# Compressed projections with both precision parts in one stationary operand, and their two halves moved among the gate groups

## The chip, the cores and the metric

The kernel runs on one core of a Trainium2 chip. The metric is the device time of one execution in microseconds; the time given is the median of three runs. TensorE multiplies, VectorE and GpSimd do elementwise work, ScalarE does activations and copies, and SyncE issues the loads of the weights.

## The reference, cut to what matters

The reference is one decoder block of two layers with 512 tokens and a model width of 1024. The change touches one piece of its sparse attention, the compressed keys and values:

```python
def compress_blocks(x, pos, w1, w2):
    ...
    blocks = jnp.concatenate([xs[:, i:i + nc] for i in range(r)], axis=2)
    blocks = blocks + pos[:, None, :]
    flat = jnp.moveaxis(blocks, 3, 2).reshape(B, nc, G, CMP_LEN * d)
    return jax.nn.gelu(flat @ w1) @ w2
```

It is called once for keys and once for values. There are 31 blocks of 32 tokens in each of 2 groups of heads with 64 channels, so `flat` has 62 rows (64 with padding) of 2048 numbers, and `w1` is 2048 x 256. What follows it on the same inputs is attention over the compressed blocks, over selected blocks and over a window, then `g_a * (ya @ w_a2d) + g_b * (yb @ w_b2d)`, whose gates `g_a` and `g_b` are sigmoids of further projections.

## The kernel before

**Precision.** A product of float32 matrices is computed in three matmuls. Every operand is split into a high part, rounded to the matmul's format, and a low part, the rest. The sum of high times high, high times low and low times high is accumulated in one bank of PSUM.

**The stream of weights.** All weight matrices lie in one stream of 128 x 128 tiles, cut into slabs of 8 tiles, in the order in which TensorE uses them (`dense_layers`, from L53). SyncE loads slab s into one of 4 raw slots (L635) as soon as slab s - 4 has been split. ScalarE rounds the slab to `w_hi` (`feed_to`, L1408 to L1416), into one of 5 slots, as soon as TensorE has used slab s - 5. Then GpSimd subtracts and gets `w_lo` (L676). From the third slab of the compressed projection on, four slabs (`DVE_SLABS`, every second one) have their `w_lo` made by VectorE instead (L2328). TensorE waits for `w_lo` at the first tile of a slab (`weight`). ScalarE's rounding is not a queue of its own: calls of `feed(name)` in ScalarE's program round all slabs up to three behind the last slab of `name`, and `after_group(name)` does that and then waits for the group's last matmul. Whatever ScalarE waits for in between holds back the slabs behind it.

**Order on TensorE around the change.** It is written out by hand (L1343 to L1347): `dense_tokens("nv", 2)`, then `compress_keys()`, `compressed(1)`, and `nsa()`.
- `compressed(b)` (L1061 to L1077) is the product `flat @ w1`, for keys (b = 0) and values (b = 1). The activations are the stationary operand: for each of 16 pairs of tiles 128 x 64 of `zc_hi` or `zc_lo`, while 256 columns of the weights move past. The output is 64 partitions x 256 columns. There are 48 matmuls for each b, 32 with `zc_hi` and 16 with `zc_lo`, over four slabs.
- `fill(p)` is a piece of work put between others: p = 0 and 1 are the halves of the gate group `gate_a0`, 2 and 3 of `gate_a1`, 4 and 5 are the groups `a2d0` and `a2d1`. Each has 12 matmuls of 512 columns. All these groups write PSUM bank 7, one after the other, and each waits until its predecessor was read: `gate_a` by a Tanh of ScalarE (`nsa_gate`, L1756), `a2d` by VectorE's `mix_down` (L2402).
- `hidden(b)` transposes the result of the Gelu, `hid_copy` moves it to SBUF, and 8 small matmuls multiply with `w2`.
- `scores`, `turn` and `values` are the steps of attention. `scores(s + 2)` waits for VectorE's `biased(s)` (`m_done`), `turn(s)` for VectorE's scaled probabilities (`p_done`).

The order is: compressed keys, fill 0, `hidden(0)`, fill 1, keys' small products, compressed values, `scores(0)`, `scores(1)`, `hidden(1)`, fill 2, values' small products, fill 3, `scores(2)`, `scores(3)`, fill 4, `turn(0)`, fill 5, and so on.

**Order on ScalarE** (L1705 to L1783): round slabs up to 30, copy the four `nv` results, `hid_gelu(0)` (which first rounds slabs 31 to 33, L1709 to L1712), round on for `gate_a0`, `hid_copy(0)`, Tanh of `gate_a0`, copy of the compressed keys, `hid_gelu(1)` with rounding before it, a one-column Exp that loads the table, `hid_copy(1)`, the exponentials of steps 0 and 1, copy of the compressed values, Tanh of `gate_a1`.

**Order on VectorE** (L2320 to L2420): `zc_lo` twice, `ya_lo` four times, the four slabs of `DVE_SLABS`, then `biased(0)` (for step 0 this is `cmp_front`: two additions from PSUM, a maximum, and the subtraction at L2345), `biased(1)`, `cmp_back(0)`, and for every step s `inverted`, `biased(s + 2)`, `scaled`, `mix_down`.

Of the kernel before, what the change touches and what calls it, by code (L numbers as in the profile page):

```python
# [19 lines left out]
ALU = mybir.AluOpType  # L20
# [33 lines left out]
def dense_layers():  # L54
# [4 lines left out]
         ("cmpk", 1, 16, 2), ("gate_a0", 1, 8, 0), ("cmpv", 1, 16, 2), ("gate_a1", 1, 8, 0)]  # L59
# [74 lines left out]
def build(nc, t):  # L134

    ctx = ExitStack()
    with ctx:
# [86 lines left out]
        zc = arena("zc", 40, [2, 16, NG, 32])  # L224
        zc_hi = arena("zc_hi", 32, [2, 16, NG, 32], F32R)
        zc_lo = arena("zc_lo", 40, [2, 16, NG, 32], F32R)
# [166 lines left out]
        hid_act = sem("hid_act")  # L393
        hid_tr = sem("hid_tr")
# [96 lines left out]
        frees("cmpk", hid_act, [1])  # L491
        frees("cmpv", hid_act, [2])
# [60 lines left out]
        first = START["cmpk"][0] // SLAB  # L553
        DVE_SLABS = range(first + 2, last_slab[START["cmpv"][1]] + 1, 2)
# [22 lines left out]
        bank_of[START["cmpk"][1]], bank_of[START["cmpv"][1]] = 3, 6  # L577
# [104 lines left out]
        def _(pe):  # L682
# [364 lines left out]
            def fill(p):  # L1047
                if p < 3 * DC:
                    m, r = p // 6 * 2, p % 6
                    if r < 4:  # L1050
                        for i in range(4 * (r % 2), 4 * (r % 2) + 4):
                            dense_part(f"gate_a{m + r // 2}", 0, i, u_hi, u_lo)
                    else:
                        for i in range(4):
                            dense_part(f"a2d{m + r - 4}", 0, i, ya_hi, ya_lo, 4)
# [5 lines left out]
            def compressed(b):  # L1061

                tile, g = START[("cmpk", "cmpv")[b]]
                pe.wait_ge(zc_ready, b + 1)
                wait_bank(g)
                out = psum[bank_of[g]][0:64, 0:256]
                for i in range(16):
                    hi, lo = weight(tile, 2)
                    zh = zc_hi[:, b, i, :, :].rearrange("p a b -> p (a b)")
                    zl = zc_lo[:, b, i, :, :].rearrange("p a b -> p (a b)")  # L1070
                    mm(out, zh, hi, start=(i == 0), stop=False)
                    mm(out, zh, lo, start=False, stop=False)
                    last = mm(out, zl, hi, start=False, stop=(i == 15))
                    tile += 2
                    if i < 15:
# [10 lines left out]
            def compress_keys():  # L1086

                compressed(0)
                fill(0)
                pe.wait_ge(nv_done, NT)  # L1090
                hidden(0)
                fill(1)
# [5 lines left out]
                last.then_inc(hid_tr, 1)  # L1098

            def compress_values():  # L1100

                hidden(1)
                fill(2)
# [6 lines left out]
                fill(3)  # L1110

            def nsa():
# [56 lines left out]
                pe.wait_ge(nv_done, 4)  # L1169
                scores(0)  # L1170
# [174 lines left out]
            compressed(1)  # L1345
            pe.wait_ge(ya_ready, 4)
# [57 lines left out]
        def _(act):  # L1404
# [294 lines left out]
            for b in range(2):  # L1699
                act.wait_ge(zc_sum, 2 * b + 2)  # L1700
                f(zc_hi[:, b, :, :, :], zc[:, b, :, :, :], ACT.Copy).then_inc(zc_part, 1)
# [80 lines left out]
            nsa_gate(3)  # L1782
# [244 lines left out]
        def _(dve):  # L2027
# [292 lines left out]
            for b in range(2):  # L2320
                dve.wait_ge(zc_part, b + 1)
                TT(zc_lo[:, b, :, :, :], zc[:, b, :, :, :], zc_hi[:, b, :, :, :].bitcast(F32), ALU.subtract)\
# [532 lines left out]
```

## Time and profile before

| | us |
|---|---|
| median of three runs | 2185.66 (2185.46 to 2186.32) |
| the profiled execution, its own time | 2185.49 |
| its span (first to last instruction) | 2183.7 |
| TensorE busy | 2145.4 |
| VectorE, ScalarE, GpSimd busy | 883.9, 878.9, 902.1 |

The profile is of one execution. All times in it are from the start of its span. A matmul's row gives its own duration, from entering to leaving the array; in a row of matmuls the distance from start to start is what one costs. An instruction's idle time stands in brackets behind it, with what ended it. The granted clock of TensorE is at its upper level (0.998 of full speed) in the mean over the whole span.

### The profile page before, as it was taken

The numbers are of one execution on the slowest core, as the hardware profiler recorded it, in microseconds if no ns is written. First come the engines' busy times: TensorE is split into PE (matmuls) and PEld (weight loads), VectorE is DVE, ScalarE is ACT, GpSimd is POOL, SyncE is SP. The second block draws the span as 40 slices with busy tenths as digits, with TensorE's granted clock in tenths as the row PEclk, the third lists the DMA queues.
The fourth block names the chain that finished last, engine by engine and source line by source line (L and its number), as shares of the span: only waits on it lengthen the run. The fifth ranks groups of instructions, "written<-read, shape, count | busy, mean of one in ns | idle before, by whom it ended". The sixth has DMA issues, their size and how long they took to land.

```text
span 2183.7 us, 27219 instructions
## 1 busy us (share of the span) xinstructions
PE 2145.4 (98%) x10960; PEld 1757.7 (80%) x10960; DVE 883.9 (40%) x1588; ACT 878.9 (40%) x1471; POOL 902.1 (41%) x385
## 2 busy tenths in 40 slices
PE   7999999999999999999999999999999999999998
PEld 6788877787788888788888888778788888888886
DVE  5494645346655500463332114653644132333211
ACT  5544655544444422452222232662346233222321
POOL 3332322245544443654444444043524444444432
PEclk9999999999999999999999999999999999999999
DMA  5222321142333333223333323023322333333321
GB/s 167 85 68 88 120 67 50 59 135 78 97 97 97 103 102 103 87 77 97 97 97 97 106 87 110 22 80 104 108 81 68 99 96 93 97 97 97 106 96 48
DMA packets 56141, 200.03 MB, mean 92 GB/s; under 512 B 6480, under 2 KB 7376, under 8 KB 55632
## 3 DMA queue, kind: packets, MB, share of 16 engines
q1 hardware_dynamic: 52416, 188.77, 28.3%
q10 hardware_dynamic: 3600, 9.53, 1.3%
q8 instruction: 87, 1.43, 0.3%
q14 instruction: 38, 0.31, 0.0%
HBM read 194.07 MB, written 2.10 MB: 90 GB/s over the span
## 4 chain that ended last, share of the span: by engine, by line
PE 92%; DVE 4%; ACT 2%; POOL 1%; issue 1%; DMA 0%; ACTq 0%; DVEq 0%
PE dense L769 16%; PE dense L771 16%; PE dense L770 16%; PE misc L769 5%; PE misc L770 5%; PE misc L771 5%; PE misc L713 3%; PE misc L715 2%; PE misc L714 2%; PE dense L749 2%; PE dense L752 2%; PE dense L753 2%; PE dense L713 1%; PE dense L715 1%; PE dense L714 1%; PE dense L1128 1%
## 5 line engine op out<-in xcount | busy, mean ns | idle before, releaser
L676 POOL TENSOR_TENSOR w_lo<-raw,w_hi 128x1024 fp32r<-128x1024 f32 x348 | 852.5, 2463 | 1161.3 <-ACT w_hi L1415 1138.2
L1415 ACT ACTIVATE w_hi<-raw 128x1024 fp32r<-128x1024 f32 x352 | 362.2, 1051 | 149.4 <-PE dense L771 87.3
L769 PE MATMUL dense<-u_hi,w_hi 128*128 128x512 f32 x848 | 333.1, 393 | 2.7 <-POOL w_lo L676 1.6
L771 PE MATMUL dense<-u_hi,w_lo 128*128 128x512 f32 x848 | 330.0, 389 | 0.0
L770 PE MATMUL dense<-u_lo,w_hi 128*128 128x512 f32 x824 | 320.7, 389 | 0.0
L769 PE MATMUL dense<-a_hi,w_hi 128*128 128x512 f32 x528 | 206.2, 391 | 0.0
L771 PE MATMUL dense<-a_hi,w_lo 128*128 128x512 f32 x528 | 205.4, 389 | 0.0
L770 PE MATMUL dense<-a_lo,w_hi 128*128 128x512 f32 x528 | 205.4, 389 | 0.0
L769 PEld LDWEIGHTS dense<-u_hi,w_hi 128*128 128x128 f32 x848 | 159.2, 188 | 38.0 <-issue 3.7
L771 PEld LDWEIGHTS dense<-u_hi,w_lo 128*128 128x128 f32 x848 | 159.2, 188 | 33.1
L770 PEld LDWEIGHTS dense<-u_lo,w_hi 128*128 128x128 f32 x824 | 154.7, 188 | 33.3 <-issue 1.4
L769 PE MATMUL misc<-u_hi,w_hi 128*128 128x512 f32 x424 | 166.0, 391 | 0.0
L771 PE MATMUL misc<-u_hi,w_lo 128*128 128x512 f32 x424 | 165.0, 389 | 0.0
L770 PE MATMUL misc<-u_lo,w_hi 128*128 128x512 f32 x416 | 161.9, 389 | 0.0
L769 PEld LDWEIGHTS dense<-a_hi,w_hi 128*128 128x128 f32 x528 | 99.1, 188 | 21.0 <-issue 0.5
L770 PEld LDWEIGHTS dense<-a_lo,w_hi 128*128 128x128 f32 x528 | 99.1, 188 | 21.0 <-issue 0.5
L771 PEld LDWEIGHTS dense<-a_hi,w_lo 128*128 128x128 f32 x528 | 99.1, 188 | 20.6
L2114 DVE SCALAR_TENSOR_TENSOR h<-dense,h 128x512 f32<-128x512 f32 x24 | 16.6, 692 | 223.7 <-PE dense L771 223.7
L2068 DVE TENSOR_TENSOR slot<-slot,slot 128x512 f32<-128x512 f32 x58 | 48.5, 837 | 135.0 <-ACT slot L1504 133.5
L1523 ACT ACTIVATE slot<-dense 128x512 f32<-128x512 f32 x30 | 17.9, 598 | 205.4 <-DVE dense L2097 205.4
L769 PEld LDWEIGHTS misc<-u_hi,w_hi 128*128 128x128 f32 x424 | 79.6, 188 | 17.1 <-issue 0.5
L771 PEld LDWEIGHTS misc<-u_hi,w_lo 128*128 128x128 f32 x424 | 79.6, 188 | 16.6
(472 smaller groups left out, 3819.3 us busy)
## 6 DMA issues: line engine op xcount, KB each, us to landing
raw<-in_weights SPq DMA_DIRECT2D x352, 512.0 KB, 3.6
h<-in_x SPq DMA_DIRECT2D x4, 512.0 KB, 5.7
alibi<-in_alibi ACTq DMA_DIRECT2D x1, 2048.0 KB, 8.6
h<-in_x ACTq DMA_DIRECT2D x2, 1024.0 KB, 6.8
out<-result SPq DMA_DIRECT2D x8, 256.0 KB, 2.2
hn<-mqk ACTq DMA_DIRECT2D x4, 256.0 KB, 4.0
mqk<-mqk ACTq DMA_DIRECT2D x4, 256.0 KB, 3.5
masks_in<-in_masks ACTq DMA_DIRECT2D x1, 512.0 KB, 4.1
```

The source lines that it names most:

```text
L676: nc.gpsimd.tensor_tensor(w_lo[:, s % SPLITS, :, :], raw[:, s % RAWS, :, :], w_hi[:, s % SPLITS, :, :].bitcast(F32), ALU.subtract).then_in ...
L713: mm(out, hi, src_hi[:, i, :], start=(i == 0), stop=False)
L714: mm(out, hi, src_lo[:, i, :], start=False, stop=False)
L715: last = mm(out, lo, src_hi[:, i, :], start=False, stop=(i == k - 1))
L749: first = mm(out, hi, src_lo[:, i, :], start=(i == 0), stop=False)
L752: mm(out, hi, src_hi[:, i, :], start=False, stop=False)
L753: last = mm(out, lo, src_hi[:, i, :], start=False, stop=(i == k - 1))
L769: mm(out, hi, src_hi[:, i, :], start=(i == 0), stop=False)
L770: mm(out, hi, src_lo[:, i, :], start=False, stop=False)
L771: last = mm(out, lo, src_hi[:, i, :], start=False, stop=(i == k - 1))
L1415: f(w_hi[:, s % SPLITS, :, :], raw[:, s % RAWS, :, :], ACT.Copy).then_inc(w_part, 1)
L2068: TT(slot[2][:, :], (slot[2] if c > 1 else sq[0])[:, :], sq[c % 3][:, :], ALU.add).then_inc(ms_acc, 1)
```

## The change

The low and high parts of the activations are put side by side: `zc_both` holds for each tile pair 64 columns of the high and 64 of the low part, and is one stationary operand of 128 x 128. Each compressed projection then has 32 matmuls, 16 with `w_hi` and 16 with `w_lo`, and its output has 128 partitions: the high part's product in partitions 0 to 63, the low part's in 64 to 127. (The product of low and low parts, left out before, is now in the sum.) ScalarE copies the lower half to `hid_low`, VectorE adds it to the upper half in PSUM, and then Gelu reads it.

The stream has each projection cut in two, `cmpk0`, `cmpk1`, `cmpv0`, `cmpv1`, two slabs each, with the gate groups between: `cmpk0`, `gate_a0`, `cmpk1`, `cmpv0`, `gate_a1`, `cmpv1`. TensorE's order follows: half keys, fill 0, fill 1, half keys, half values, `hidden(0)`, fill 2, keys' small products, fill 3, half values, `scores(0)`, `scores(1)`, two of the four tiles of fill 4, `hidden(1)`, `scores(2)`, `scores(3)`, values' small products, the other two tiles of fill 4, `turn(0)`, fill 5 and so on. ScalarE's and VectorE's orders change as shown.

```diff
-         ("cmpk", 1, 16, 2), ("gate_a0", 1, 8, 0), ("cmpv", 1, 16, 2), ("gate_a1", 1, 8, 0)]
+         ("cmpk0", 1, 8, 2), ("gate_a0", 1, 8, 0), ("cmpk1", 1, 8, 2), ("cmpv0", 1, 8, 2), ("gate_a1", 1, 8, 0),
+          ("cmpv1", 1, 8, 2)]
...
-        zc = arena("zc", 40, [2, 16, NG, 32])
-        zc_hi = arena("zc_hi", 32, [2, 16, NG, 32], F32R)
-        zc_lo = arena("zc_lo", 40, [2, 16, NG, 32], F32R)
+        zc = arena("zc", 16, [2, 16, NG, 32])
+        zc_both = arena("zc_both", 32, [2, 16, 2, NG, 32], F32R)
+        hid_low = arena("hid_low", 64, [2, 256])
...
-        first = START["cmpk"][0] // SLAB
-        DVE_SLABS = range(first + 2, last_slab[START["cmpv"][1]] + 1, 2)
+        first = START["cmpk0"][0] // SLAB
+        DVE_SLABS = range(first + 2, last_slab[START["cmpv1"][1]] + 1, 2)
...
-            def fill(p):
+            def fill(p, tiles=range(4)):
...
-                        for i in range(4):
+                        for i in tiles:
                             dense_part(f"a2d{m + r - 4}", 0, i, ya_hi, ya_lo, 4)
...
-            def compressed(b):
-
-                tile, g = START[("cmpk", "cmpv")[b]]
-                pe.wait_ge(zc_ready, b + 1)
-                wait_bank(g)
-                out = psum[bank_of[g]][0:64, 0:256]
-                for i in range(16):
+            def compressed(b, half):
+
+                tile, g = START[("cmpk", "cmpv")[b] + str(half)]
+                if half == 0:
+                    pe.wait_ge(zc_ready, b + 1)
+                    wait_bank(g)
+                out = psum[bank_of[g]][:, 0:256]
+                for i in range(8 * half, 8 * half + 8):
                     hi, lo = weight(tile, 2)
-                    zh = zc_hi[:, b, i, :, :].rearrange("p a b -> p (a b)")
-                    zl = zc_lo[:, b, i, :, :].rearrange("p a b -> p (a b)")
-                    mm(out, zh, hi, start=(i == 0), stop=False)
-                    mm(out, zh, lo, start=False, stop=False)
-                    last = mm(out, zl, hi, start=False, stop=(i == 15))
+                    z = zc_both[:, b, i, :, :, :].rearrange("p a b c -> p (a b c)")
+                    mm(out, z, hi, start=(i == 0), stop=False)
+                    last = mm(out, z, lo, start=False, stop=(i == 15))
...
-                compressed(0)
+                compressed(0, 0)
                 fill(0)
+                fill(1)
+                compressed(0, 1)
+                compressed(1, 0)
                 pe.wait_ge(nv_done, NT)
                 hidden(0)
-                fill(1)
+                fill(2)
                 pe.wait_ge(hid_done, 1)
...
                 last.then_inc(hid_tr, 1)
+                fill(3)
+                compressed(1, 1)

             def compress_values():

-                hidden(1)
-                fill(2)
                 pe.wait_ge(hid_done, 2)
...
-                fill(3)
...
                 scores(0)
                 scores(1)
-                compress_values()
-                pe.wait_ge(kvc_copied, 2)
+                fill(4, range(2))
+                hidden(1)
                 for first in range(0, SLOTS, 2):
                     if first + 2 < SLOTS:
                         scores(first + 2)
                         scores(first + 3)
                     alone = first % 9 == 0
+                    if first == 0:
+                        compress_values()
                     for s in (first, first + 1):
                         if s < SLOTS - 1:
-                            fill(pieces_of(s)[0])
+                            fill(pieces_of(s)[0], range(2, 4) if s == 0 else range(4))
+                        if s == 0:
+                            pe.wait_ge(kvc_copied, 2)
                         turn(s)
...
             def hid_gelu(b):
-                name = ("cmpk", "cmpv")[b]
+                name = ("cmpk1", "cmpv1")[b]
                 after_group(name)
+                f(hid_low[0:64, b, :], out_bank(name)[64:128, 0:256], ACT.Copy).then_inc(hid_moved, 1)
+                act.wait_ge(hid_sum, b + 1)
                 f(hid_t[0:64, b, :], out_bank(name)[0:64, 0:256], ACT.Gelu_apprx_tanh).then_inc(hid_act, 1)
...
+            feed("gate_a0")
+            nsa_gate(1)
+            f(spare_col, one_col, ACT.Gelu_apprx_tanh)
             hid_gelu(0)
-            feed("gate_a0")
+            feed("cmpv0")
             hid_copy(0)
-            nsa_gate(1)
             act.wait_ge(hid_tr, 2)
             f(kc[:, :], misc[0][:, 0:32], ACT.Copy).then_inc(kvc_copied, 1)
+            nsa_gate(3)
             hid_gelu(1)
...
-            nsa_gate(3)
             nsa_feed(1)
...
+            def hid_add(b):
+
+                dve.wait_ge(hid_moved, b + 1)
+                out = out_bank(("cmpk1", "cmpv1")[b])[0:64, 0:256]
+                TT(out, out, hid_low[0:64, b, :], ALU.add).then_inc(hid_sum, 1)
+
             for s in DVE_SLABS:
+                if s > last_slab[START["cmpv0"][1]] and s - 2 <= last_slab[START["cmpv0"][1]]:
+                    hid_add(0)
                 dve.wait_ge(w_part, s + 1)
...
+            hid_add(1)
             dve.wait_ge(c_loaded, 80)
             biased(0)
```

## Rows read from the trace of the kernel before

**Rows 1.** The page, busy time of each engine, and the chain that ended last:

```profile
PE 2145.4 (98%) x10960; PEld 1757.7 (80%) x10960; DVE 883.9 (40%) x1588; ACT 878.9 (40%) x1471; POOL 902.1 (41%) x385
...
PE 92%; DVE 4%; ACT 2%; POOL 1%; issue 1%; DMA 0%; ACTq 0%; DVEq 0%
```

**Rows 2.** Timeline of TensorE: start and duration in us, instruction, [idle before <- releaser]:

```profile
223.32 0.28 PE L788 MATMUL misc<-w_hi,u_hi 128*128 128x256 f32 x1
...
234.83 0.28 PE L1071 MATMUL dense<-w_hi,zc_hi 128*64 128x256 f32 x1
...
238.84 0.33 PE L1071 MATMUL dense<-w_hi,zc_hi 128*64 128x256 f32 x1 [1.12 <-DVE w_lo L2328]
...
242.27 0.47 PE L713 MATMUL misc<-u_hi,w_hi 128*128 128x512 f32 x1 [0.47 <-DVE w_lo L2328]
...
248.94 0.33 PE L1071 MATMUL misc<-w_hi,zc_hi 128*64 128x256 f32 x1
...
254.53 1.08 PE L1122 MATMUL dense<-kc,nq 64*128 64x31 f32 x16
...
255.75 0.28 PE L1083 MATMUL misc<-ident,hid_t 64*128 64x64 f32 x2
...
258.92 0.63 PE L1107 MATMUL misc<-w,hid 128*32 128x64 f32 x8
...
263.18 0.50 PE L713 MATMUL misc<-ya_hi,w_hi 128*128 128x512 f32 x1
...
266.03 1.03 PE L1141 MATMUL misc<-ident,c_s 128*31 128x128 f32 x8
266.97 0.50 PE L713 MATMUL misc<-ya_hi,w_hi 128*128 128x512 f32 x1
```

**Rows 3.** Timeline of ScalarE, same columns, from slab 33 to slabs 35 to 38:

```profile
242.48 1.06 ACT L1415 ACTIVATE w_hi<-raw 128x1024 fp32r<-128x1024 f32 x1 [4.55 <-DMA raw<-in_weights]
243.56 1.28 ACT L1712 ACT_TABLE_LOAD   x1
244.85 0.38 ACT L1712 ACTIVATE hid_t<-dense 64x256 f32<-64x256 f32 x1
...
248.69 0.60 ACT L1756 ACTIVATE gate_t<-misc 128x512 f32<-128x512 f32 x1 [2.35 <-PE misc L715]
...
249.26 4.07 ACT L1415 ACTIVATE w_hi<-raw 128x1024 fp32r<-128x1024 f32 x4
```

**Rows 4.** Timeline of VectorE, same columns, first steps of attention:

```profile
255.73 0.48 DVE L2340 TENSOR_TENSOR c_s<-dense,c_bias 128x124 f32<-128x124 f32 x2 [4.16 <-PE dense L1122]
...
256.69 2.10 DVE L2345 TENSOR_TENSOR c_s<-c_s,st 128x248 f32<-128x248 f32 x1
...
259.27 0.41 DVE L2352 TENSOR_REDUCE st<-c_s 128x8 f32<-128x248 f32 x1
...
260.94 0.16 DVE L2381 RECIPROCAL st<-st 128x2 f32<-128x2 f32 x1
262.96 0.29 DVE L2371 CUSTOM_DVE_ANT_0 n_s<-dense,alibi 128x128 f32<-128x128 f32 x1 [1.86 <-PE dense L1128]
...
263.39 0.60 DVE L2392 TENSOR_SCALAR n_s<-n_s,st,small 128x128 f32<-128x128 f32 x2
266.23 0.69 DVE L2402 SCALAR_TENSOR_TENSOR mix_t<-gate_t,misc 128x512 f32<-128x512 f32 x1 [2.24 <-PE misc L715]
```

**Rows 5.** Two lines of VectorE: durations in ns (least, median, most), first and last start:

```profile
L2328 DVE TENSOR_TENSOR w_lo<-raw,w_hi x4: 1224/2318/3439, 235.4 to 250.3; 128x1024 fp32r<-128x1024 f32 x4
...
L2345 DVE TENSOR_TENSOR c_s<-c_s,st x4: 417/1094/2102, 256.7 to 374.9; 128x248 f32<-128x248 f32 x4
```

**Rows 6.** Timeline of GpSimd, slab 34:

```profile
246.26 2.40 POOL L676 TENSOR_TENSOR w_lo<-raw,w_hi 128x1024 fp32r<-128x1024 f32 x1 [5.21 <-ACT w_hi L1415]
```

**Rows 7.** Timelines of GpSimd and VectorE, from 523 to 538 us:

```profile
527.59 10.37 POOL L676 TENSOR_TENSOR w_lo<-raw,w_hi 128x1024 fp32r<-128x1024 f32 x4 [4.42 <-ACT w_hi L1415]
...
523.64 9.71 DVE L2068 TENSOR_TENSOR slot<-slot,slot 128x512 f32<-128x512 f32 x7
```

More of the change, by code:

```diff
@@ L393, in build @@
         hid_act = sem("hid_act")
+        hid_moved = sem("hid_moved")
+        hid_sum = sem("hid_sum")
         hid_tr = sem("hid_tr")
@@ L490, in build @@
         frees("nv", nv_done, [1, 2, 3, 4])
-        frees("cmpk", hid_act, [1])
-        frees("cmpv", hid_act, [2])
+        for b in range(2):
+            frees(f"cmpk{b}", hid_act, [1])
+            frees(f"cmpv{b}", hid_act, [2])
         for m in range(DC):
@@ L576, in build @@
             bank_of[START["nv"][1] + c] = 4 + c
-        bank_of[START["cmpk"][1]], bank_of[START["cmpv"][1]] = 3, 6
+        for b in range(2):
+            bank_of[START[f"cmpk{b}"][1]], bank_of[START[f"cmpv{b}"][1]] = 3, 6
         for name in ("up", "up1", "up2"):
@@ L1059, in fill @@
                         dense_part(f"gate_b{m}", 0, i, u_hi, u_lo)
-            def compressed(b):
-                tile, g = START[("cmpk", "cmpv")[b]]
-                pe.wait_ge(zc_ready, b + 1)
-                wait_bank(g)
-                out = psum[bank_of[g]][0:64, 0:256]
-                for i in range(16):
-                    hi, lo = weight(tile, 2)
-                    zh = zc_hi[:, b, i, :, :].rearrange("p a b -> p (a b)")
-                    zl = zc_lo[:, b, i, :, :].rearrange("p a b -> p (a b)")
-                    mm(out, zh, hi, start=(i == 0), stop=False)
-                    mm(out, zh, lo, start=False, stop=False)
-                    last = mm(out, zl, hi, start=False, stop=(i == 15))
+            def compressed(b, half):
[5 more added lines that the diff above has]
+                for i in range(8 * half, 8 * half + 8):
+                    hi, lo = weight(tile, 2)
+                    z = zc_both[:, b, i, :, :, :].rearrange("p a b c -> p (a b c)")
+                    mm(out, z, hi, start=(i == 0), stop=False)
+                    last = mm(out, z, lo, start=False, stop=(i == 15))
                     tile += 2
-                    if i < 15:
+                    if i % 8 < 7:
                         used(last, tile - 1)
@@ L1169, in nsa @@
                 pe.wait_ge(nv_done, 4)
+                pe.wait_ge(ya_ready, 4)
                 scores(0)
                 scores(1)
-                compress_values()
-                pe.wait_ge(kvc_copied, 2)
+                fill(4, range(2))
+                hidden(1)
                 for first in range(0, SLOTS, 2):
@@ L1344, in _ @@
             compress_keys()
-            compressed(1)
-            pe.wait_ge(ya_ready, 4)
             nsa()
@@ L1700, in _ @@
                 act.wait_ge(zc_sum, 2 * b + 2)
-                f(zc_hi[:, b, :, :, :], zc[:, b, :, :, :], ACT.Copy).then_inc(zc_part, 1)
+                f(zc_both[:, b, :, 0, :, :], zc[:, b, :, :, :], ACT.Copy).then_inc(zc_part, 1)
             for hd in range(GH):
@@ L2321, in _ @@
                 dve.wait_ge(zc_part, b + 1)
-                TT(zc_lo[:, b, :, :, :], zc[:, b, :, :, :], zc_hi[:, b, :, :, :].bitcast(F32), ALU.subtract)\
+                TT(zc_both[:, b, :, 1, :, :], zc[:, b, :, :, :], zc_both[:, b, :, 0, :, :].bitcast(F32), ALU.subtract)\
                     .then_inc(zc_ready, 1)
@@ L2739, in layout @@
         "ncmp": np.concatenate([kcm, vcm], 1),
-        "nv": np.concatenate([vsl, vwi], 1), "cmpk": one("cmp_w1_k"), "cmpv": one("cmp_w1_v"),
+        "nv": np.concatenate([vsl, vwi], 1),
+        "cmpk0": one("cmp_w1_k")[:D], "cmpk1": one("cmp_w1_k")[D:],
+        "cmpv0": one("cmp_w1_v")[:D], "cmpv1": one("cmp_w1_v")[D:],
         "w_o": one("w_o"), "up": pairs(up[:, :FF], up[:, FF:]), "down": one("w_down"),
```

## The prediction

> **What bounds the kernel now.** I read the page first. TensorE is busy 98% of the span and 92% of the chain that ended last is its own work [rows 1]. So a microsecond off TensorE's own stream counts in full, but so does every new wait in that stream. The sum is made on the profiled execution: span 2183.7 us, time 2185.49 us, which is 0.17 us under the median of 2185.66 us. An effect in that one stretch is carried to the median unchanged. 0.2% of it is 4.4 us, about what a measurement of this kernel can tell from no change.
>
> Then the stretch that the edit touches, from the first compressed matmul at 234.83 us to the point where the second `a2d` group starts, 266.97 us: 32.14 us [rows 2]. Behind that point the order of the work is the old one. TensorE's timeline shows what a matmul costs there: with 128 stationary columns 96 matmuls of 256 moving columns take from 223.32 to 234.83 us, 0.120 us each; with 64 stationary columns 48 of them take from 248.94 to 254.53 us, 0.116 us each with the gap behind, 0.114 us from start to start. It idles 1.12 us at 238.84 and 0.47 us at 242.27 us, both for a `w_lo` slab that VectorE makes [rows 2]. Everything else in the stretch is back to back.
>
> Last the engines that feed it, because the change moves their work too. ScalarE rounds a slab in 1.06 us, or four in 4.07, and loads a table for Gelu in 1.28 us, between slab 33 at 242.48 and the Gelu at 244.85 us [rows 3]. GpSimd makes a `w_lo` slab in 2.4 us [rows 6], VectorE one in 1.22 us at best and in 3.4 us at worst, beside GpSimd [rows 5]. In the old numbering slabs 27 to 30 are `cmpk`, 31 `gate_a0`, 32 to 35 `cmpv`, 36 `gate_a1`, 37 the first two `a2d`. In the new one 27 and 28 are `cmpk0`, 29 `gate_a0`, 30 and 31 `cmpk1`, 32 and 33 `cmpv0`, 34 `gate_a1`, 35 and 36 `cmpv1`, 37 as before. VectorE's slabs stay 29, 31, 33 and 35.
>
> **What goes.** 96 matmuls at 0.114 us become 64 at 0.120 us: 10.94 less 7.68, a saving of 3.3 us. That a full-width stationary costs double is excluded by the 0.120 us [rows 2]. With it the wait of 0.47 us goes, as slab 31 is now needed after a whole gate group.
>
> **What comes, as a clock.** Up to 242 us nothing ahead of ScalarE, VectorE and GpSimd has changed, so old times hold for slabs 29 to 32.
> - 234.83: `cmpk0`, 16 matmuls, to 236.75. Slab 29 is ready at 238.79, as now; TensorE waits 2.1 us, 0.8 more than now (counted from start to start). `gate_a0`, 24 matmuls of 512 columns with 0.23 us each ([rows 2]: 12 take 2.85 us from 263.18 to 266.03), to 244.4; its result is whole at 244.65.
> - `cmpk1` and slab 32 of `cmpv0`, 24 matmuls, to 247.3.
> - ScalarE now issues `feed("gate_a0")`, which ends with slab 32, and then stands in the wait of `nsa_gate(1)` until 244.65. Slab 33, rounded at 242.48 now [rows 3], is queued behind it. Tanh 0.6, to 245.3; table load for the spare Gelu 1.28, to 246.6; slab 33 from 246.7 to 247.75; slab 34 to 248.7. Only an extra load for Tanh stands ahead of its wait, in idle time. VectorE makes slab 33 by 249.0. TensorE waits **1.7 us**, then does its 8 matmuls to 250.0.
> - The halves: ScalarE's copy of 64x256, 0.39 (the Gelu of the same shape, [rows 3]), VectorE's addition some 0.35 (between 0.24, half of the `c_s<-dense` pair of 124 columns, and 0.69, `mix_t` with 512 columns, both with a PSUM operand, [rows 4]), Gelu 0.39: done about 249.8, covered by `cmpv0`. Without that cover it would cost 1.1 us.
> - Slab 34 (`gate_a1`) is GpSimd's: from 248.75 to 251.15. TensorE is through the two transposes at 250.3 and waits **0.9 us**. Two fills and the 8 small products of the keys take it to 257.25; `gate_a1` is whole at 257.4. `cmpv1` to 259.2, its slabs being ready. `scores(0)` and `(1)`, 1.22 us (254.53 to 255.75, [rows 2]), to 260.4.
> - ScalarE waits in `nsa_gate(3)` until 257.4; Tanh to 258.0; then slabs 37, 38 and 39 to 260.95, before it copies the lower half of `cmpv1`. GpSimd makes slab 37 from 259.1 to 261.5: TensorE waits **1.1 us** for it. Half of `a2d0` and the two transposes, to 263.3.
> - VectorE adds the halves at 261.65 and only then starts `biased(0)`, which now runs at 255.73 [rows 4]: 0.96 us to the subtraction `c_s<-c_s,st`. This reads SBUF twice; at 256.69 it took 2.10 us beside GpSimd [rows 4], against 0.42 us at best [rows 5]. Here it waits for slab 38, until 263.9, and ends at 264.2. `scores(2)` needs it: TensorE waits **0.9 us**. `scores(2)` and `(3)`, the values' products (0.63), the other half of `a2d0`: to 267.15.
> - `biased(1)` 0.5, to 264.75; `cmp_back(0)` takes 1.67 us (259.27 to 260.94, [rows 4]) and is held once more by slab 39, until 266.6: done 267.65. `turn(0)` waits **0.5 us** for it.
> - `inverted(1)`, `biased(2)`, `scaled(1)` 1.2 us (0.16, and 262.96 to 263.99, [rows 4]), then `mix_t` of `a2d0` 0.69: 269.45. The second `a2d` group needs that bank: TensorE, through `turn(0)` at 268.6, waits **0.8 us**.
>
> So the second `a2d` group starts at 269.45, not 266.97: **2.5 us later**. As a check: 3.3 and 0.5 saved; 0.8, 1.7, 0.9, 1.1, 0.9, 0.5 and 0.8 added, 6.7 in all, less 3.8, is 2.9. I take the clock. Buffers: the two raw and split rings have the same slots, and by the clock no load is late, since slab 33's has landed by 242.48 and the others start when the slab four before is split.
>
> ScalarE's load takes 1.28 us and its next instruction follows at once: load at 243.56, Gelu at 244.85 [rows 3]. The Trainium skill (ScalarE: Activation LUTs, "What ACT_TABLE_LOAD costs") adds a drain of 1.38 us to each switch, 2.66 us in all; by it slab 33 would come 1.4 us later and the kernel be at 2189.5. The trace does not agree, and the sum keeps 1.28.
>
> **The rivals.**
> - *The saving arrives.* If ScalarE's slabs 33, 34 and 37 are not needed as early as I have them, only slab 29's wait stays: 3.3 and 0.5 less 0.8, 3.0 us faster, 2182.7. For it: the new order is easier on the feed per matmul, and GpSimd has idle time, 5.21 us before slab 34 [rows 6]. Against: ScalarE's instruction order is fixed, and slab 33 stands behind Tanh in it.
> - *No table load between Tanh and slab 33*, since now Tanh runs at 248.69 in Gelu's table without a load [rows 3]. The set that serves Tanh first may be that one. Then everything from slab 33 on is 1.4 us earlier: +1.1, 2186.8.
> - *Slower.* VectorE's subtraction at 262.6 meets GpSimd with slab 39 queued right behind slab 38. If GpSimd keeps the access, VectorE starts at 266.3, 2.4 us later, and so do `turn(0)` and all behind it: +4.9, 2190.6. It decides once ScalarE rounds slab 39 before 263.9; by the clock it does. Against: around 530 us VectorE's `slot<-slot,slot` got in between two of GpSimd's four queued slabs, which then took 10.37 us in place of four times 2.4 [rows 7]. By the Trainium skill (SBUF — State Buffer, "Who interferes with whom") whoever issues first holds the shared port for the whole instruction; the trace agrees, with 2.10 us for the subtraction of 0.42.
>
> **How the numbers follow.** Forecast 0.60, saving arrives 0.12, no load 0.13, slower 0.15. The likeliest gives 2185.66 + 2.5 = 2188.2 us. The terms that no row gives exactly (addition 0.24 to 0.69, load 0 or 1.28, one hand-over of 2.4) span -1.4 to +2.4 about it, 2186.8 to 2190.6. I put the range at 2184.6 to 2190.9: it leaves out the first rival and what lies beyond the last. Faster by over 0.2% would need more than the whole saving: 0.02. Slower by over 0.2% is the last rival: 0.15. The rest, 0.83, is within 0.2%.
>
> **What would show it.** After: 32 matmuls of each compressed projection, 0.120 us apart; TensorE idle some 2 us before `gate_a0`, 1.7 us inside `cmpv0` for VectorE's slab, 0.9 us before `gate_a1` and 1.1 us before `a2d0`, both for GpSimd's; ScalarE's slab 33 starting near 246.7, behind Tanh and a table load; `biased(0)` not before 261 us. The forecast is wrong if slab 33 is rounded before Tanh, if TensorE does not wait in `cmpv0`, or if the second `a2d` group starts before 266.5 us.

## The result, and the profile after

The changed kernel takes 2196.64 us (median of 5 runs, 2195.32 to 2197.04) against 2185.58 us (5 runs, 2184.99 to 2186.32): 11.06 us more, a ratio of 1.0048 [1.0037, 1.0059]. Forecast was 2188.2 us, between 2184.6 and 2190.9. The profiled execution took 2197.04 us with a span of 2195.2 us, the one before 2183.7 us.

The page after, the same two lines as [rows 1]:

```profile
PE 2148.4 (98%) x10928; PEld 1759.4 (80%) x10928; DVE 883.9 (40%) x1590; ACT 881.1 (40%) x1475; POOL 902.7 (41%) x385
...
PE 92%; DVE 4%; ACT 2%; POOL 1%; issue 1%; DMA 0%; ACTq 0%; DVEq 0%
```

There are 32 matmuls fewer, as the change says, and yet TensorE is busy 3.0 us longer. The other 8.5 of the 11.5 us by which the span is longer are idle time. Shares of the span can't tell where; three views do. The first is a yardstick that both kernels have: the moments at which ScalarE rounds each of the 352 slabs. The kernel after lags the one before by 0.75 us at slab 28 (ahead of any changed instruction), 4.43 at slab 40, then by the same until slab 112, 9.48 at slab 118, 11.27 at slab 200, 12.23 at slab 230, 11.56 at slab 300 and to the end. So the changed stretch cost 3.7 us, and 7.1 us were lost in steps of 5.1, 1.8, 1.0 and -0.7 in places that the diff doesn't touch. The second view names them: what TensorE waited for from 700 to 1900 us, before,

```profile
engine line waited for: us in total, times, longest us
PE misc L1210 <- ACT w_pt L1878: 1.3, 2, 0.8
PE dense L788 <- ACT r_raw L1934: 1.0, 1, 1.0
```

and after, in the same stretch:

```profile
engine line waited for: us in total, times, longest us
PE dense L774 <- DVE slot L2479: 3.2, 1, 3.2
PE dense L774 <- DVE slot L2114: 1.5, 1, 1.5
PE misc L1221 <- ACT w_pt L1891: 1.3, 2, 0.8
...
PE dense L741 <- issue: 0.8, 1, 0.8
```

The line for `w_pt` has its twin before. The other three, for L774 twice and for L741, have none: they are new. TensorE's timeline after, start and duration in us, with the idle time ahead in brackets:

```profile
239.66 0.47 PE L718 MATMUL misc<-u_hi,w_hi 128*128 128x512 f32 x1 [1.99 <-DVE w_lo L2349]
...
251.40 0.39 PE L1076 MATMUL misc<-w_hi,zc_both 128*128 128x256 f32 x1 [1.54 <-DVE w_lo L2349]
...
253.73 0.47 PE L718 MATMUL misc<-u_hi,w_hi 128*128 128x512 f32 x1 [0.84 <-POOL w_lo L681]
...
264.18 0.47 PE L718 MATMUL misc<-ya_hi,w_hi 128*128 128x512 f32 x1 [0.93 <-POOL w_lo L681]
...
271.45 0.50 PE L718 MATMUL misc<-ya_hi,w_hi 128*128 128x512 f32 x1 [0.29 <-DVE mix_t L2423]
...
756.23 0.39 PE L776 MATMUL dense<-u_hi,w_lo 128*128 128x512 f32 x1
...
759.79 0.79 PE L774 MATMUL dense<-a_hi,w_hi 128*128 128x512 f32 x1 [3.17 <-DVE slot L2479]
...
1191.02 0.50 PE L774 MATMUL dense<-a_hi,w_hi 128*128 128x512 f32 x1 [1.51 <-DVE slot L2114]
1311.83 0.47 PE L741 MATMUL dense<-u_hi,w_hi 128*128 128x512 f32 x1 [0.83 <-issue]
```

The first five are the waits of the changed stretch, and they answer to the forecast's clock. (The row at 756.23 us has no wait; it is the last matmul of `up`.) The last three are not in it at all: the first matmuls of `down`, of `down1` and of the `wq` part. Ahead of `down` the kernel before went straight on:

```profile
751.81 0.39 PE L771 MATMUL dense<-u_hi,w_lo 128*128 128x512 f32 x1
752.03 0.39 PE L769 MATMUL dense<-a_hi,w_hi 128*128 128x512 f32 x1
```

The reason is one line of the code that the diff does not touch, `bank_of = [g % 4 for g in range(GROUPS)]`: a group's PSUM bank comes from its number. The change cuts `cmpk` and `cmpv` into two groups each, so every group behind them has a number that is two higher and, where the code gives it no bank by hand, sits two banks away from its old one. The up projection in front of `down` doesn't move: its 44 groups count their own six banks (`c % 6`). Before, `down`'s first group took over bank 3, last used by group 39 of `up`; now it takes bank 1, that of group 43, the last one, and so waits for VectorE's last step of the convolution (L2479). Before, the four groups of `up` that came behind group 39 covered that step. `down1` meets the same behind `up1`. The first group of `wq` has bank 0 by hand; before, it took that bank over from the third last group of `down1`, now from the last one. The row of its wait names no releaser, but the wait comes and goes with the banks in the first two experiments.

The third view, windows at four moments (us, then busy time and count of instructions of PE, PEld, DVE, ACT and POOL, then PEclk, DMA share, GB/s):

```profile
189.78:193.20 3.42, 3.42 (x18) 3.42 (x18) 0.23 (x1) 2.33 (x4) 3.42 (x2) 0.50 0.58 150
240.98:244.40 3.42, 3.42 (x10) 2.65 (x9) 1.85 (x1) 0.00 (x0) 0.76 (x1) 0.50 0.93 304
264.88:268.29 3.41, 3.41 (x18) 2.33 (x18) 2.86 (x9) 2.73 (x8) 3.41 (x2) 0.50 0.72 189
759.81:763.22 3.41, 3.41 (x8) 2.73 (x9) 1.82 (x3) 0.78 (x2) 0.00 (x0) 0.50 0.00 0
```

The granted clock is 0.50 in each: TensorE runs at 1.2 instead of 2.4 GHz. Three of the four falls begin within 1.4 us behind a wait of the timeline above (1.99, 0.93 and 3.17 us). The first stands in unchanged code, and TensorE waited at most 0.23 us at a time in the 5 us ahead of it. Eight matmuls fill 3.41 us from 759.81 us, 0.43 us each. In the kernel before, at full clock, 63 of them fill 14 us there, 0.22 us each:

```profile
752.00:766.00 14.00, 14.00 (x63) 11.59 (x62) 8.21 (x8) 7.73 (x10) 6.49 (x3) 1.00 0.39 122
```

This fall therefore costs 8 times 0.21, 1.7 us. A fall costs less where it takes the place of a wait. The one at 189.78 us is why the slabs lag by 0.75 us at slab 28 (at slab 27 they do not lag yet): of its 1.3 us of longer matmuls, 0.5 went into a wait that only the kernel before has:

```profile
192.13 0.38 PE L999 MATMUL dense<-u_new,kt_t 128*128 128x128 f32 x1 [0.52 <-ACT u_new L1662]
```

The longer matmuls count as busy time, which is how TensorE can be busy longer with fewer of them. Counted up to the same matmul in both kernels, TensorE was busy 1.2 us longer ahead of the changed stretch, 1.0 behind it, 2.9 behind the fall at 759.81 us and 3.0 at the end. So in the changed stretch its two falls, and what five waits cost beyond their idle time, used up the 3.3 us saved. The profile before shows no fall while TensorE has work.

Two theories stand for the first experiments. By the one, the waits behind the changed stretch come from the banks alone, whatever the order. By the other, the new order itself delays what follows, and the waits near 756 and 1188 us go with it.

### The profile page after: what moved, and what is told of

Read it like the earlier page. It is cut to its first block, busy times and chain, and to the rows that moved or that the text cites. A ratio compares the mean times of both kernels' runs of the same rounds, so it can differ in the third digit from the quotient of the medians.

```text
span 2195.2 us, 27161 instructions
## 1 busy us (share of the span) xinstructions
PE 2148.4 (98%) x10928; PEld 1759.4 (80%) x10928; DVE 883.9 (40%) x1590; ACT 881.1 (40%) x1475; POOL 902.7 (41%) x385
## 4 chain that ended last, share of the span: by engine, by line
PE 92%; DVE 4%; ACT 2%; POOL 1%; issue 1%; DMA 0%; ACTq 0%; DVEq 0%
PE dense L774 16%; PE dense L776 16%; PE dense L775 16%; PE misc L776 5%; PE misc L775 5%; PE misc L774 5%; PE misc L718 3%; PE misc L720 2%; PE misc L719 2%; PE dense L754 2%; PE dense L758 2%; PE dense L757 2%; PE dense L718 1%; PE dense L720 1%; PE dense L719 1%; PE dense L1134 1%
## 5 line engine op out<-in xcount | busy, mean ns | idle before, releaser
L774 PE MATMUL dense<-u_hi,w_hi 128*128 128x512 f32 x848 | 333.2, 393 | 2.7 <-POOL w_lo L681 1.6
L774 PE MATMUL dense<-a_hi,w_hi 128*128 128x512 f32 x528 | 207.2, 392 | 4.7 <-DVE slot L2479 3.2
L774 PEld LDWEIGHTS dense<-u_hi,w_hi 128*128 128x128 f32 x848 | 159.2, 188 | 37.9 <-issue 3.7
L774 PE MATMUL misc<-u_hi,w_hi 128*128 128x512 f32 x424 | 166.0, 391 | 0.0
L774 PEld LDWEIGHTS dense<-a_hi,w_hi 128*128 128x128 f32 x528 | 99.5, 188 | 26.5 <-DVE slot L2479 3.6
L774 PEld LDWEIGHTS misc<-u_hi,w_hi 128*128 128x128 f32 x424 | 79.6, 188 | 17.1 <-issue 0.5
```

The costliest lines, as they stand in the source:

```text
L774: mm(out, hi, src_hi[:, i, :], start=(i == 0), stop=False)
```

## The experiments

The kernel before, run beside them on the same chips, took 2186.00 us (26 runs) with the first four, 2186.07 (31 runs) with the next four, 2186.03 (29 runs) with the last four.

### The old banks, with the whole change

```diff
-        bank_of = [g % 4 for g in range(GROUPS)]
+        bank_of = [(g - 2 * (g > START["cmpv1"][1])) % 4 for g in range(GROUPS)]
```

> The changed kernel, with the PSUM banks of all groups behind the compressed ones numbered as in the kernel before. Bank theory: the 3.2 us wait of TensorE before the first matmul of down at 760 us and the 1.5 us one before down1 at 1191 us come from the group numbers that moved by two, which put these groups into the bank that the last up group still holds. Then both waits go, with the clock drop behind the first, and the time falls by the 7.2 us that the kernel loses after 460 us: 2189.4 us. Rival, chance in the placing of later work (instruction supply, clock): the waits stay, 2196.6 us.

Measured: 2189.74 us (10 runs), 1.0018 [1.0008, 1.0027]. The waits of `down`, `down1` and `wq` are gone, and the lag at the slabs stays at 4.1 us from slab 40 to the end. So of the 11.06 us lost 3.7 are left, and 7.3 came from the banks. The ten runs lie in three groups, 2187.37 and 2187.8, four at 2189.03 to 2189.93, four at 2191.0 to 2191.9, whose means lie 1.9 and 2.0 us apart, near the price of a fall. That reads as runs with none, one and two, but only one of them has a profile: the falls of the others are argued from their times. The profiled execution, 2189.55 us, is of the middle group and has one fall, behind the waits before `gate_a0`, in `cmpv0` and before `gate_a1`:

```profile
252.28:255.69 3.41, 3.41 (x9) 2.65 (x9) 0.44 (x1) 0.14 (x1) 2.61 (x1) 0.50 0.78 259
```

Its timeline of TensorE, from 264 us on, shows what the kernel after hides under its slower clock:

```profile
266.32 0.38 PE L1134 MATMUL dense<-nk,nq 64*128 64x128 f32 x2 [0.63 <-DVE c_s L2366]
...
269.56 0.27 PE L1147 MATMUL misc<-ident,c_s 128*31 128x128 f32 x1 [0.17 <-DVE c_s L2378]
...
271.07 0.50 PE L718 MATMUL misc<-ya_hi,w_hi 128*128 128x512 f32 x1 [0.47 <-DVE mix_t L2423]
```

From the first compressed matmul to the second `a2d` group it takes 35.76 us with this one fall, and the kernel after takes 35.86 us with two: its fall at 264.88 us took the place of the first two of these waits and of part of the third, and cost about 0.1 us. So falls can't simply be counted at 1.7 us each.

### The new banks, with nothing else

```diff
-        bank_of = [g % 4 for g in range(GROUPS)]
+        bank_of = [(g + 2 * (g > START["cmpv"][1])) % 4 for g in range(GROUPS)]
```

This is the kernel before, with each later group in the bank that the change gives it.

> The kernel before, with nothing but the group numbers behind the compressed groups moved by two for the choice of banks. Bank theory: it loses what the changed kernel loses after 460 us, some 7 us, 2192.8 us, with waits of about 3 us before down and 1.5 us before down1. Rival (the waits need the changed stretch): 2185.6 us.

Measured: 2193.4 us (5 runs), 1.0034 [1.0021, 1.0047], 7.4 us more than the kernel before. Without one instruction of the change, both waits are there, at their full length:

```profile
756.10 0.78 PE L769 MATMUL dense<-a_hi,w_hi 128*128 128x512 f32 x1 [3.17 <-DVE slot L2457]
...
1187.37 0.50 PE L769 MATMUL dense<-a_hi,w_hi 128*128 128x512 f32 x1 [1.51 <-DVE slot L2101]
```

The theory of the order falls. Its profile has the fall behind `down`'s wait too. The fastest of the five, 2192.11 us, has a mean granted clock of 0.999 where the others have 0.997; it is 6.1 us above the kernel before, so most of the 7.4 us is waiting and not clock. The 7.4 us here and the 3.7 us of the old banks' run are 11.1, the whole loss of 11.06.

### TensorE kept busy in the wait for slab 29

The old banks, plus 16 matmuls of 256 columns into an unused bank where TensorE waits for slab 29.

```diff
+                for _ in range(16):
+                    mm(bank[1][:, 0:256], zc_both[:, 0, 0, :, :, :].rearrange("p a b c -> p (a b c)"), u_hi[:, 0, 0:256],
+                       start=True, stop=True)
```

> As e1_old_banks, with 16 matmuls of 256 columns into an unused bank in the place where TensorE idles 2 us for slab 29; their result is not used. Clock theory: the granted clock does not fall at 241 us, gate_a0 runs at 0.23 us a matmul throughout, and the time is 1.7 to 1.9 us under e1_old_banks (2187.6 us). Rival, the clock falls for another reason than the idle time, or the fall is covered by the wait for slab 33 behind it: no difference to e1_old_banks, or less than 0.5 us.

Measured: 2189.09 us (10 runs), 0.65 us under the old banks' run and not 1.7: a miss as a median. The group with two falls is gone (none over 2189.58), but only one run, at 2187.56, is in the group with none, and the profiled one has a fall at 251.4 us. Three runs, at 2188.34 to 2188.56, lie between the groups. Keeping this one wait filled removes at most one of the falls.

### VectorE makes slab 29 first

The old banks; VectorE splits slab 29 ahead of the four `ya_lo` steps instead of behind them.

```diff
+            slab_lo(DVE_SLABS[0])
             for hd in range(GH):
                 head_lo(hd)
...
-            for s in DVE_SLABS:
+            for s in DVE_SLABS[1:]:
```

> As e1_old_banks, with VectorE making slab 29 ahead of the four ya_lo subtractions in place of behind them. My clock: slab 29 is ready before TensorE asks, the 2.0 us wait and the 1.8 us of low clock behind it go, and all waits behind move up with it, as their producers hang on gate_a0: 3.8 us under e1_old_banks, 2185.6 us. Rival, the later waits (slab 33 behind Tanh, slab 37, biased) take it back since they hang on loads and GpSimd: 1 us or less.

Measured: 2187.5 us (10 runs), 1.0002 [0.9993, 1.0012]. That is 2.2 us under the old banks' run where 3.8 were expected: a miss as a median. Four runs are at 2184.87 to 2185.32, near the 2185.6 us expected, and six at 2187.32 to 2188.2. The wait before `gate_a0` is gone; those for ScalarE's slabs 33 and 34 (1.54 and 0.85 us) stay, and behind them the profiled run has a fall to 0.50 of 6.83 us, from 248.33 us on, twice as long as the others.

### ScalarE ahead of Tanh

Now the step that the forecast made the main one: slab 33 behind Tanh. On top of the last edit, ScalarE issues the slabs of `cmpk1`'s feed and the spare Gelu before it stands in the wait for `gate_a0`.

```diff
-            feed("gate_a0")
-            nsa_gate(1)
             f(spare_col, one_col, ACT.Gelu_apprx_tanh)
+            feed("cmpk1")
+            nsa_gate(1)
```

> As e4_slab29_first, with ScalarE loading Gelu's table and rounding slabs 33 and 34 ahead of the Tanh of gate_a0 in place of behind it. Queue theory (slab 33 is late because it stands behind the Tanh and a table load in ScalarE's program): the waits of 1.54 us inside cmpv0 and 0.85 us before gate_a1 both go, 2.4 us under the undisturbed runs of e4 (2185.1): 2182.7 us, and the clock has no idle time of over a microsecond to fall on. Rival, slab 33 is late through its load or through VectorE: the 1.54 us stays, 2185 to 2187.5 us.

Measured: 2183.11 us (10 runs), 0.9986 [0.9977, 0.9996]. Both waits are gone, 0.94, 0.65, 0.18 and 0.47 us are left, and the runs lie in one group, 2182.41 to 2184.01 us. (Three of them have a mean granted clock of 0.997 and are no slower than the rest.) Against the lower group of the run before this is 2.1 us less, about the two waits' 2.4; against its median it is 4.4. The difference fits the clock, which does not fall in this profile.

### ScalarE ahead of the second gate too

On top of the last edit, slabs 37 and 38 are rounded ahead of the Tanh of `gate_a1`.

```diff
-                after_group(name)
+                if b == 0:
+                    after_group(name)
+                else:
+                    act.wait_ge(dense_done, group_of(name))
...
+            feed_to(last_slab[START["cmpv1"][1]] + 3)
             nsa_gate(3)
```

> As e5_scalar_ahead, with slabs 37 and 38 rounded ahead of the Tanh of gate_a1, and slab 39 behind the Gelu of the values. Queue theory: the waits of 0.94, 0.65, 0.18 and 0.47 us behind cmpv1 (slab 37, the subtraction of the compressed scores, turn(0), the bank of a2d1) go as well, another 2.2 us: 2180.5 us, 5 us under the kernel before. Rival, the copy, addition and Gelu of two halves are a chain that holds up biased(0) whatever is ahead of it: the waits on VectorE stay, 1 us or less gained over e5.

Measured: 2180.9 us (10 runs), 0.9977 [0.9968, 0.9986]. ScalarE rounds slabs 31 to 34 and only then meets its Tanh:

```profile
236.83 1.28 ACT L1783 ACT_TABLE_LOAD   x1
...
238.24 2.94 ACT L1424 ACTIVATE w_hi<-raw 128x1024 fp32r<-128x1024 f32 x3
243.26 1.06 ACT L1424 ACTIVATE w_hi<-raw 128x1024 fp32r<-128x1024 f32 x1 [2.08 <-PE misc L720]
244.22 0.58 ACT L1770 ACTIVATE gate_t<-misc 128x512 f32<-128x512 f32 x1
```

In the window over these matmuls TensorE's busy time is the window itself, at full clock:

```profile
235.50:262.19 26.69, 26.69 (x183) 22.44 (x181) 14.62 (x30) 17.20 (x35) 14.95 (x6) 1.00 0.65 198
```

From 234 to 280 us one wait is left, the one for `a2d1`'s bank that was expected to go too. In total, times and longest:

```profile
PE misc L718 <- DVE mix_t L2431: 0.5, 1, 0.5
```

### The operand alone

The kernel before with only the shared operand, the copy and the addition of the halves; groups, order and banks as before.

```diff
-                    mm(out, zh, hi, start=(i == 0), stop=False)
-                    mm(out, zh, lo, start=False, stop=False)
-                    last = mm(out, zl, hi, start=False, stop=(i == 15))
+                    mm(out, z, hi, start=(i == 0), stop=False)
+                    last = mm(out, z, lo, start=False, stop=(i == 15))
```

> The kernel before, old order and old groups, with only the operand changed: 32 matmuls with 128 stationary columns for each projection, halves copied and added. My sum: the keys' saving goes into the wait for slabs 29 and 31, which stay ready at 238.8 and 242.1 us, the values keep 1.6 us: 2184.4 us, or about 2186 with a fall of the clock behind the longer wait at 238.8 us. Rival, TensorE saves all of it: 3.3 us, 2182.7 us. Rival, the chain of copy, addition and Gelu is on the path in hidden(1): 2186 to 2187 us without any fall of the clock.

Measured: 2186.0 us (10 runs), 0.9999 [0.9989, 1.0008]. The 3.3 us saved turn into waits:

```profile
239.45 0.39 PE L1072 MATMUL dense<-w_hi,zc_both 128*128 128x256 f32 x1 [1.91 <-DVE w_lo L2338]
...
242.88 0.47 PE L715 MATMUL misc<-u_hi,w_hi 128*128 128x512 f32 x1 [1.25 <-DVE w_lo L2338]
...
246.32 0.24 PE L1083 MATMUL misc<-ident,hid_t 64*128 64x64 f32 x1 [0.44 <-ACT hid_t L1714]
...
255.76 0.27 PE L1083 MATMUL misc<-ident,hid_t 64*128 64x64 f32 x1 [0.48 <-ACT hid_t L1714]
```

The first two grew from 1.12 and 0.47 us [rows 2], 1.6 us more; the other two are the chain of copy, addition and Gelu with nothing over it, 0.9 us. Together 2.5 of the 3.3. In this profile, which has no fall of the clock, the stretch is 0.6 us shorter than before, 31.58 against 32.14 us; the median shows nothing of it. The ten runs spread over 2.1 us, and the two slowest have a mean granted clock of 0.996 where the profiled one has 0.999.

### Slab 29 first, in the kernel before

The kernel before, without the change, and VectorE's slab 29 ahead of `ya_lo`.

```diff
+            slab_lo(DVE_SLABS[0])
             for hd in range(GH):
                 head_lo(hd)
-            for s in DVE_SLABS:
+            for s in DVE_SLABS[1:]:
+                slab_lo(s)
```

> The kernel before with VectorE making slab 29 ahead of ya_lo, nothing else. The 1.12 us wait at 238.8 us goes, with a quarter of a microsecond of restart; the one of 0.47 us before gate_a0 grows to about a microsecond since TensorE comes there earlier and slab 31 is made behind ya_lo: 2185 to 2185.7 us, against 2186.0. Rival, slab 31 moves up by as much: 2184.2 us.

Measured: 2186.57 us (10 runs), 1.0002 [0.9993, 1.0011]: a miss, since 0.3 to 1 us less was expected and it is 0.5 more. The wait for slab 29 went and that for slab 31 grew from 0.47 to 1.83 us, for the same line of VectorE. Its timeline shows why:

```profile
233.77 1.22 DVE L2326 TENSOR_TENSOR w_lo<-raw,w_hi 128x1024 fp32r<-128x1024 f32 x1
234.90 6.92 DVE L2318 TENSOR_TENSOR ya_lo<-o_t,ya_hi 128x512 fp32r<-128x512 f32 x4
```

The four `ya_lo` steps took 2.49 us in the kernel before, ahead of the slabs:

```profile
232.94 2.49 DVE L2318 TENSOR_TENSOR ya_lo<-o_t,ya_hi 128x512 fp32r<-128x512 f32 x4
```

Now, beside GpSimd's slabs, they take 6.92 us, and the slab that is needed next stands behind them. That is why nothing was won: in this profile the stretch takes 31.97 us, 0.2 less than before. The 0.5 us more of the median are not in it. Three of the ten runs, the slowest, have a mean granted clock of 0.997 where the others have 0.999.

### Banks mixed

The kernel with ScalarE ahead of both gates, with `out` and what follows in their new banks and all between in the old ones.

```diff
-        bank_of = [(g - 2 * (g > START["cmpv1"][1])) % 4 for g in range(GROUPS)]
+        bank_of = [(g - 2 * (START["cmpv1"][1] < g < START["out"][1])) % 4 for g in range(GROUPS)]
```

> As e6_all_ahead, with the new bank numbers from the group out on (out, up2, down2) and the old ones ahead of it. Bank theory in the other direction: the 0.33 us wait of the kernel before for the sum of its last out chunk, at 1811 us ahead of up2, goes, and with it the 0.66 us that the changed kernel won back there: 2180.2 us. Rival, that gain hung on the other shifts: 2180.9 us.

Measured: 2180.36 us (8 runs), 0.9974 [0.9963, 0.9984]: the fastest of all, 5.7 us under the kernel before and 16.3 under the change. The kernel before waits a little where `up2` takes over a bank from `out`,

```profile
1811.02 0.50 PE L736 MATMUL dense<-u_hi,w_hi 128*128 128x512 f32 x1 [0.33 <-DVE h L2114]
```

and with the new banks this wait is gone, here and in the kernel after. Read at the slabs that is worth 0.7 us, as expected; the medians differ by 0.5.

### The order alone

The old banks and the new order, but the old operand: 48 matmuls with 64 stationary columns, no halves to add. The copy and the addition go as well; their lines are shown with the next run.

```diff
-                    mm(out, z, hi, start=(i == 0), stop=False)
-                    last = mm(out, z, lo, start=False, stop=(i == 15))
+                    mm(out, zh, hi, start=(i == 0), stop=False)
+                    mm(out, zh, lo, start=False, stop=False)
+                    last = mm(out, zl, hi, start=False, stop=(i == 15))
```

> As e1_old_banks, with the old operand: 48 matmuls with 64 stationary columns per projection, nothing copied or added. This is the new order alone. Queue theory: TensorE has 3.3 us more to do, but nearly all of it goes into the waits for slabs 29, 33, 34 and 37, and the chain to biased(0) is shorter by copy and addition: 2188.5 to 2190 us, like e1 (2189.7). Rival, the operand's saving counts in full in this order: 2193 us.

Measured: 2187.86 us (10 runs, 2187.03 to 2188.41), 1.0008 [0.9999, 1.0018], 0.6 us below what was expected. With more matmuls to do, TensorE comes later to each slab and waits less for it:

```profile
239.05 0.47 PE L718 MATMUL misc<-u_hi,w_hi 128*128 128x512 f32 x1 [1.18 <-DVE w_lo L2341]
...
249.18 0.33 PE L1077 MATMUL misc<-w_hi,zc_both 128*64 128x256 f32 x1 [0.33 <-DVE w_lo L2341]
```

In place of 1.96, 1.54, 0.84 and 0.93 us there are 1.18, 0.33, 0.48 and none. So in this order, at full clock, the operand is worth next to nothing: 2187.86 without it, 2187.6 with it in the two runs read as without a fall. With it the median is 2189.74, a loss. That the longer waits bring the falls fits, but no run shows why the clock falls.

### The order, fed ahead, with the old operand

The edit of the last section, on the kernel with ScalarE ahead of both gates. The lines of the copy, which went in the last section too:

```diff
-                f(hid_low[0:64, b, :], out_bank(name)[64:128, 0:256], ACT.Copy).then_inc(hid_moved, 1)
-                act.wait_ge(hid_sum, b + 1)
```

> As e6_all_ahead, with the old operand as in e10. With the feed ahead there is no wait to take the extra work: 3.3 us more than e6, 2184.2 us. Rival, the feed still binds: less than 2 us more.

Measured: 2184.25 us (10 runs), 0.9991 [0.9982, 1.0]. Against the same kernel with the operand, 2180.9, it is 3.35 us: exactly the 3.3 us of the forecast's first term, once nothing in the feed is late.

### The wait for slab 29 put back

The kernel with ScalarE ahead of both gates, with VectorE's slab 29 behind `ya_lo` again.

```diff
-            slab_lo(DVE_SLABS[0])
             for hd in range(GH):
                 head_lo(hd)
-            for s in DVE_SLABS[1:]:
+            for s in DVE_SLABS:
```

> As e6_all_ahead, with VectorE's slab 29 behind ya_lo again. The only thing put back is TensorE's 2.1 us wait ahead of gate_a0. Clock theory: single runs fall into two groups, those whose clock stays up at about 2183.0 us, and those where it falls behind the wait 1.7 us higher. Rival without the clock: one group at 2183.0 us. Rival, the lost 2.1 us are caught up behind: 2181 us.

Measured: 2183.14 us (10 runs, 2182.61 to 2183.9), 0.9986 [0.9977, 0.9995], one group. The wait is back and costs a little more than its length, 2.2 us, in the median and in the profile (from the first compressed matmul to the second `a2d` group 29.27 against 27.05 us):

```profile
239.48 0.47 PE L718 MATMUL misc<-u_hi,w_hi 128*128 128x512 f32 x1 [1.98 <-DVE w_lo L2343]
```

The window over the stretch, at full clock:

```profile
234.00:270.00 36.00, 33.55 (x222) 28.03 (x221) 17.39 (x46) 22.56 (x50) 15.68 (x7) 1.00 0.43 147
```

But the second group, 1.7 us higher, that the clock theory wanted did not come in ten runs: the expectation of the clock theory is a miss. With the old banks alone, where waits of 1.54, 0.84 and 0.93 us follow this one within 25 us, eight of ten runs lie in the groups with a fall. But waits close together do not always bring one either: the profile of the operand alone has 1.91, 1.25 and 0.44 us within 7 us and no fall.

## Why the prediction was wrong, point by point

- **"Behind that point the order of the work is the old one."** This is the step that failed. The order is the old one, the banks are not: the new group numbers moved every later group by two banks, and that is 7.4 us of the 11.06 by itself (new banks alone) and 7.3 taken back by the one-line remedy. The forecast counted the groups (it needed their new numbers for the slabs) and did not ask what else reads that number.
- **The saving, 3.3 us.** Right in size (3.35 us where the feed is ahead), and as forecast it did not arrive in the change.
- **Slab 29, 2.1 us before `gate_a0`.** Measured 1.99. **Slab 33, 1.7 us inside `cmpv0`.** 1.54. **Slab 34, 0.9 before `gate_a1`.** 0.84. **Slab 37, 1.1 before `a2d0`.** 0.93. Each for the engine that was named.
- **ScalarE's order as the cause of 1.7 us.** Right. ScalarE's timeline after (0.75 us later than the forecast's clock through the fall at 189.78 us) reads Tanh, table load, slab 33, as the forecast had them:

```profile
247.03 0.60 ACT L1767 ACTIVATE gate_t<-misc 128x512 f32<-128x512 f32 x1 [7.07 <-PE misc L720]
247.64 1.28 ACT L1782 ACT_TABLE_LOAD   x1
248.94 0.20 ACT L1782 ACTIVATE small<-small 128x1 f32<-128x1 f32 x1
249.05 1.99 ACT L1424 ACTIVATE w_hi<-raw 128x1024 fp32r<-128x1024 f32 x2
251.06 0.38 ACT L1721 ACTIVATE hid_low<-dense 64x256 f32<-64x256 f32 x1
```

  From Tanh to slab 33 it is 2.02 us, where the forecast had 2.05; both come 1.6 us later than on the shifted clock, by the fall at 240.98 us, which delays `gate_a0` as well and so leaves the wait as it was. Moving the feed ahead of Tanh removed this wait and the next.
- **The rival without a table load** is out by the line at 247.64 us. The load takes 1.28 us and the next instruction starts at 248.94, right behind it. By the Trainium skill (ScalarE: Activation LUTs, "What ACT_TABLE_LOAD costs") a drain of 1.38 us comes on top; this trace again doesn't show it, and keeping it out of the sum was right.
- **The addition of the halves, some 0.35 us.** Measured 0.42 us, on VectorE; covered, as said, in the new order, and not covered in the old one (0.9 us in the operand's run alone).
- **`scores(2)` 0.9, `turn(0)` 0.5, the bank of the second `a2d` group 0.8.** With the old banks 0.63, 0.17 and 0.47: right places, sizes by 0.3 us too large each. The slower rival's hand-over to slab 39 did not come: the subtraction took 1.45 us after, not 2.10, and `scores(2)` did not wait for it there.

```profile
264.27 0.46 DVE L2361 TENSOR_TENSOR c_s<-dense,c_bias 128x124 f32<-128x124 f32 x2
265.21 1.45 DVE L2366 TENSOR_TENSOR c_s<-c_s,st 128x248 f32<-128x248 f32 x1
```

- **The stretch in all, 2.5 us.** With the old banks it takes 35.76 us against 32.14 before, 3.6 more with one fall in it, so some 1.9 us without; the two runs read as without a fall give 1.6 us (2187.6 against 2186.0). The mechanism was right and the terms together 0.6 to 0.9 us too large.
- **The clock had no term.** The waits that were forecast bring falls that were not: the median with the old banks is 3.7 us above the kernel before, so about 2 us are the clock's, one fall in a typical run. It is still inside the range given. The fall behind `down`'s wait is part of the banks' 7.4.

With the banks left alone the forecast, 2188.2 us, would have been 1.5 us low, and that only because terms that were too large stood against a fall that had no term: in part luck. With the banks it was 8.4 us low.

## What to carry to other kernels

When a change alters how many groups, tiles or buffers there are, look up everything that is computed from their running number (banks, ring slots, engines by parity) and ask of each later hand-over whose work it now waits for; here that was worth twice the whole local effect. A saving on the bounding engine arrives only as far as its feeders are ahead: here 3.35 us with ScalarE's slabs issued before it stands in a wait, nothing with them behind. A kernel that is bound by TensorE can also pay more for an idle stretch than its length: 2.2 us for 1.98 here, and up to 1.7 us more in executions where the clock fell behind it. So give short waits that bunch a margin above their sum.

## What the hardware showed that was not expected

- TensorE's clock fell to half behind waits of 0.8 to 3.2 us in some executions of a kernel and not in others. By the groups of their times, the same 1.98 us wait before `gate_a0` came with no fall in ten runs where it stood alone, and with one or two in eight of ten where waits of 1.54, 0.84 and 0.93 us followed. Each fall in a profile but one lasted 3.41 us, that one 6.83 us. One of 3.41 us cost from about 0.1 us, where it took the place of waits, to 1.7 us. Falls at 189.5 or 189.8 us stand in the profiles of three kernels (the change, the new banks alone, the feed all ahead) in code that none of them changed. What decides whether it falls stays open.
- Four `ya_lo` steps of VectorE took 6.92 us beside GpSimd. By the Trainium skill (SBUF — State Buffer, "Who interferes with whom") an operation of VectorE with two inputs in SBUF shares a read port with GpSimd and one of the two is locked out; the trace agrees: beside GpSimd, busy for 5.2 of the 6.92 us, they took that long, and 2.49 us with GpSimd idle for all but the last 0.6 us. For a queue this means that an instruction moved away from such a collision may hand it to the next one.
